# One retention / conformer / ConvFFN layer on one core: the opening goes by pairs of channel tiles, with the conditioning weights stationary, and VectorE takes 40 low parts of weights

## What is computed

```
mod  = silu(cond) @ ada_w + ada_b            # 6 x 1024 numbers for c, 6 x 1024 for c_ctx
h    = rms_norm(x, n1_pre) * (1 + sc1) + sh1 # scale and shift: the first 2 x 1024 columns of ada_w
proj = h @ w_in                              # q k v g | u_a u_b | two gates
ret  = bidirectional retention(q, k, v), per-head GroupNorm, silu(g) * ., @ ret_w_out
conv = depthwise conv 31 over u_a * sigmoid(u_b), LayerNorm, silu, @ conv_w_out
x    = x + g1 * rms_norm((sig * ret + sig * conv) @ w_mix_out, n1_post)
h2   = rms_norm(x, n2_pre) * (1 + sc2) + sh2
up   = depthwise conv 3 (h2 @ ffn_w_up);  x = x + g2 * rms_norm((silu(a) * gl) @ ffn_w_down, n2_post)
```

## Time and profile before

| | us |
|---|---|
| median of 3 runs | 2124.91 (2122.43 to 2125.99) |
| the profiled execution | 2129.53 |
| its span | 2127.7 |
| PE busy | 2082.3 (98%) |
| DVE busy | 1681.1 (79%) |
| POOL busy | 963.2 (45%) |
| ACT busy | 827.5 (39%) |

### The profile page before, as it was taken

One profiled execution on the slowest core, in us unless ns is written; L12 is line 12 of the kernel. 1 busy time (PEld: TensorE's weight loads), 2 busy tenths in 40 slices (PEclk: granted clock), 3 DMA queues, 4 the chain that ended last, 5 costly groups with the idle time before them and its releaser, 6 DMA issues.

```text
span 2127.7 us, 30742 instructions
## 1 busy us (share of the span) xinstructions
PE 2082.3 (98%) x12055; PEld 1880.9 (88%) x12055; DVE 1681.1 (79%) x1906; ACT 827.5 (39%) x1378; POOL 963.2 (45%) x597
## 2 busy tenths in 40 slices
PE   7999999999999999999999999999999999999998
PEld 3888887887887899999999998899999999978886
DVE  3599899899899687787536546599989989868867
ACT  3512212212212366665547333343433333344344
POOL 1445635645645366665381230036666566570000
PEclk9999999999999999999999999999999999999999
DMA  9342442442432455544464444312323223258453
GB/s 306 119 143 91 138 130 85 138 134 84 137 104 91 162 160 170 173 148 155 166 225 148 132 159 147 113 33 63 93 63 90 66 63 93 75 196 297 139 178 114
DMA packets 233760, 283.08 MB, mean 133 GB/s; under 512 B 11441, under 2 KB 176145, under 8 KB 233617
## 3 DMA queue, kind: packets, MB, share of 16 engines
q1 hardware_dynamic: 180785, 212.41, 31.7%
q10 hardware_dynamic: 51424, 63.98, 9.0%
q0 software_dynamic: 1408, 4.72, 0.6%
HBM read 214.06 MB, written 67.01 MB: 132 GB/s over the span
## 4 chain that ended last, share of the span: by engine, by line
PE 84%; DVE 9%; ACT 2%; issue 1%; DMA 1%; SPq 1%; POOL 1%; ACTq 0%; DVEq 0%; POOLq 0%
PE ps L1130 82%; DVE conv_y L2586 2%; DVE f_cv L2921 1%; DVE T_raw L2876 1%; SPq L766 1%; PE ps L1345 1%; DMA x_all<-in_x_sample 1%; DVE T_lo L2902 1%; DMA r_raw<-rT_d 0%; PE ps L1393 0%; DMA sh_row<-gain_d 0%; DVE Al L2960 0%; ACT sq_t L1668 0%; DVE x_all L2529 0%; PE ps L1184 0%
## 5 line engine op out<-in xcount | busy, mean ns | idle before, releaser
L2586 DVE SCALAR_TENSOR_TENSOR conv_y<-u_in,VC,conv_y 128x1167 f32<-128x1167 f32 x240 | 482.0, 2010 | 10.6 <-ACT conv_y L1759 3.6
L1130 PE MATMUL ps<-A_hi,Wa_hi 128*128 128x384 f32 x768 | 261.4, 340 | 0.5 <-DVE A_lo L2543 0.5
L2288 POOL TENSOR_TENSOR Wa_lo<-W_raw,Wa_hi 128x1024 fp32r<-128x1024 f32 x58 | 156.7, 2708 | 225.8 <-ACT Wa_hi L1637 225.7
L1130 PE MATMUL ps<-A_hi,Wa_lo 128*128 128x384 f32 x768 | 258.9, 337 | 0.0
L1130 PE MATMUL ps<-A_lo,Wa_hi 128*128 128x384 f32 x768 | 258.7, 337 | 0.0
L2921 DVE SCALAR_TENSOR_TENSOR f_cv<-f_in,VF,f_cv 128x1023 f32<-128x1023 f32 (+1 forms) x176 | 212.9, 1260 | 1.8
L2440 POOL TENSOR_TENSOR O_lo<-E,O_hi 128x512 fp32r<-128x512 f32 x80 | 130.2, 1628 | 152.6 <-ACT O_hi L1637 152.6
L2440 POOL TENSOR_TENSOR O_lo<-F_raw,O_hi 128x512 fp32r<-128x512 f32 x68 | 112.2, 1652 | 145.2 <-ACT O_hi L1637 145.2
L1130 PE MATMUL ps<-Wb_hi,A_lo 128*128 128x512 f32 x432 | 169.8, 393 | 0.0
L1130 PE MATMUL ps<-Wb_hi,A_hi 128*128 128x512 f32 x432 | 169.6, 393 | 0.0
L1130 PE MATMUL ps<-Wb_lo,A_hi 128*128 128x512 f32 x432 | 169.4, 392 | 0.0
(11 more groups left out here) (338 smaller groups left out, 5533.5 us busy)
## 6 DMA issues: line engine op xcount, KB each, us to landing
F_raw<-in_ffn_w_up SPq DMA_DIRECT2D x44, 512.0 KB, 5.6
qt<-qkvg_d SPq DMA_DIRECT2D x36, 512.0 KB, 3.6
W_raw<-in_w_in SPq DMA_DIRECT2D x32, 512.0 KB, 4.8
W_raw<-in_w_in SPq DMA_DIRECT2D x64, 256.0 KB, 3.3
ada_w<-in_ada_w ACTq DMA_DIRECT2D x30, 512.0 KB, 4.0
F_raw<-in_ffn_w_down SPq DMA_DIRECT2D x30, 512.0 KB, 4.9
A_raw<-g_d SPq DMA_DIRECT2D x25, 512.0 KB, 4.3
g_d<-f_cv SPq DMA_DIRECT2D x22, 576.0 KB, 3.6
```

The lines of the kernel that those rows point to most:

```text
L1130: return pe.matmul(out, l, r, start=start, stop=stop)
L2288: return pool.tensor_tensor(dst, x, Fv(hi), ALU.subtract)
L2586: dve.scalar_tensor_tensor(out=y, in0=x, scalar=tap, in1=y, op0=ALU.mult, op1=ALU.add).then_inc(q.conv_step, 1)
```

## The change

**Conditioning.** `ada_p` is now stationary: for one channel tile k and one of shift or scale, 8 products of 128x128 weights with `cs` (2 columns) give the column of `mod` straight in PSUM. 16 such columns make 128 products in place of 64, and `mod_row`, its copies and its turns go. It is done by pairs p of channel tiles: `ada_early(p)` is 32 products. The weights of a pair come as two DMAs of 1 MB (scale, then shift).

**Order of the steps.** A pair has 6 steps: three thirds of x times two channel tiles (`step_of`). Each step multiplies with chunk 0 and chunk 1 at once. `ada_early(p + 1)` stands after the third step of pair p. The squares and the norming of thirds 1 and 2 stand ahead of steps 2 and 4 on ACT and DVE, and `x_turn(j + 2)` ahead of the products of step j on PE. All turns use one PSUM bank, and ACT writes to three SBUF buffers; DVE makes all high and low parts.

**Queues.** SP: c, third 0 of x, chunks 0 and 1, pair 0, thirds 1 and 2, pairs 1 to 3, chunks 2 to 5. The 13 small loads go from SP to ACT's queue, behind the Silu. The exponentials of the decay go behind the splits of chunks 0 and 1.

**Low parts.** VectorE makes 40 that POOL made: chunks 6i+2 to 6i+5 for i = 1 to 7 (for odd i between taps of tile i - 1, for even i after them), and operands o = 0 to 11 of the FFN. POOL's other low parts wait for these by the counter.

```diff
-            def ada_early(n):
...
-                    last = mm(ps[0:2, n // 2, (n % 2) * 256:(n % 2 + 1) * 256], cs[:, k, :], ada_p[:, n, k, :], k == 0, k == KT - 1)
...
+            def ada_early(p):
+
+                if p:
+                    pe.wait_ge(q.mod_ok, p)
+                for v in (SC1, SH1):
+                    pe.wait_ge(*ada_piece_in(v, p))
+                    for k in (2 * p, 2 * p + 1):
+                        c = 2 * (v * KT + k)
+                        for r in range(KT):
+                            last = mm(ps[:, MOD_BANK, c:c + 2], ada_p[:, v * KT + r, k * P:(k + 1) * P], cs[:, r, :], r == 0, r == KT - 1)
+                        last.then_inc(q.ada_used, 1)
...
+                for j in range(N_A):
+                    while turned < min(j + 3, N_A):
+                        x_turn(turned)
+                        turned += 1
+                    if j < N_A - 2:
+                        for e in range(2):
...
+                            product(e, j)
+                    if j % PER_PAIR == PER_PAIR - 4 and j // PER_PAIR + 1 < N_PAIR:
+                        ada_early(j // PER_PAIR + 1)
...
             for j in range(N_A):
+                if j % PER_PAIR == 0:
+                    act.wait_ge(q.mod_ok, j // PER_PAIR + 1)
+                if j in (2, 4):
+                    squares(j // 2)
                 modulated(j)
...
+                    if i % 2 == 0 and w in LO_TAPS:
+                        if w == LO_TAPS[0]:
+                            dve.wait_ge(q.w_lo, 6 * (i + 1) + 2)
+                        lo_w(6 * (i + 1) + 2 + LO_TAPS.index(w))
...
+                    if i + 1 < KT:
+                        dve.wait_ge(q.w_lo, 6 * (i + 1) + 2)
+                        for e in range(2, 6):
+                            lo_w(6 * (i + 1) + e)
```

More of the change, by code:

```diff
@@ L826, in chunk_load @@
                                      w_in_s[:, 2 * j:2 * j + 2, 2 * g + s, h * 256:(h + 1) * 256]).then_inc(done, 16)
-            for n in range(4, 7):
-                ada_chunk(n)
             chunk_load(0)
-            ada_chunk(7)
+            chunk_load(1)
+            ada_pair(0)
             x_load(1)
-            chunk_load(1)
             sp.wait_ge(x_in[0], X_IN[0])
@@ L835, in _ @@
             sp.dma_start(x_all[:, NL, :], a["x_prompt"][0]).then_inc(x_in[2], 16)
+            for p in range(1, N_PAIR):
+                ada_pair(p)
             for n in range(2, 6):
@@ L1151, in row_turns @@
                 pe.wait_ge(q.vec_ok, 1)
-                pe.transpose(ps[:, 7, 0:120], rows[0:120, 0, :], ident[0:120, 0:120]).then_inc(q.vecT, 1)
+                pe.transpose(ps[:, ROW_BANK, 0:120], rows[0:120, 0, :], ident[0:120, 0:120]).then_inc(q.vecT, 1)
                 pe.transpose(ps[:, 5, 0:88], rows[0:88, 1, :], ident[0:88, 0:88]).then_inc(q.vecT, 1)
@@ L1205, in ada_part @@
                     last.then_inc(q.ada_used, 1)
[L1206 to L1217, removed]
-            def first_u():
[L1222 to L1243, removed]
@@ new lines, in _, with product @@
+            row_turns()
+            ada_early(0)
+            def first_u():
+                turned = 0
+                pe.wait_ge(q.vec_ok, 6)
+                def product(e, j):
+                    g, k = step_of(j)
+                    tiles = slice(3 * g, 3 * g + 3)
+                    o = ps[:, 3 * e + g, 0:TG].rearrange("p (t n) -> p t n", n=P)
+                    wh, wl = (x[chunk_slot(e)].rearrange("p (k n) -> p k n", k=KT) for x in (w_hi, w_lo))
+                    pe.wait_ge(q.hT_lo, j + 1)
+                    mm(o, wh[:, k, :], A_hi[:, tiles, k, :], k == 0, False)
+                    mm(o, wh[:, k, :], A_lo[:, tiles, k, :], False, False)
+                    return mm(o, wl[:, k, :], A_hi[:, tiles, k, :], False, k == KT - 1)
+                for j in range(N_A):
[4 more added lines that the diff above has]
+                        for e in range(2):
+                            if j == 0:
+                                pe.wait_ge(q.w_lo, e + 1)
+                            product(e, j)
+                    if j % PER_PAIR == PER_PAIR - 4 and j // PER_PAIR + 1 < N_PAIR:
+                        ada_early(j // PER_PAIR + 1)
+                for e in range(2):
+                    for j in (N_A - 2, N_A - 1):
+                        last = product(e, j)
+                    last.then_inc(q.u_ps, 1)
@@ L2315, in _ @@
                 h, g = divmod(i, 2)
-                for e in range(2, 6):
-                    if i:
-                        lo_w(6 * i + e)
                 if i:
@@ L2566, in _, with mods @@
-            for j in range(N_A):
-                if j == 3:
-                    normed(1)
-                if j == 8:
-                    meaned(2)
-                    normed(2)
+            decay_tables()
+            def mods(p):
+                dve.wait_ge(q.ada_used, 4 * (p + 1))
+                dve.wait_ge(q.vec_ok, 2)
+                two = slice(2 * p, 2 * p + 2)
+                for v in (SH1, SC1):
+                    r = v * KT + 2 * p
+                    c = 2 * r
+                    ins = dve.tensor_tensor(mod[:, r:r + 2, :], ps[:, MOD_BANK, c:c + 4].rearrange("p (k c) -> p k c", c=2),
+                                            col2(V_ADAB + r, 2), ALU.add)
+                then(ins)
+                dve.scalar_tensor_tensor(out=hscale[:, two, :], in0=mod[:, SC1 * KT + 2 * p:SC1 * KT + 2 * p + 2, :], scalar=1.0,
+                                         in1=col2(V_N1PRE + 2 * p, 2), op0=ALU.add, op1=ALU.mult).then_inc(q.mod_ok, 1)
@@ L3082, in _ @@
             t_op(R4, R4, b_of(B_lo, 1, 0), ALU.add)
+            for x in (U_S2, U_S3, U_A22):
+                op_lo(op_no(PLAIN, x))
             T_lo_part(2)
```

224 lines of the change are left out of this document (110 added, 114 removed).

## The result

The changed kernel takes 2164.32 us (median of 5 runs, 2161.51 to 2166.35) against 2125.51 of the kernel before beside it: **1.0182 times the time, 95% interval 1.0170 to 1.0194**, 38.8 us more. The forecast was 2131.1, with a range up to 2152.

The account below looks back on a forecast made before the run. PE, busy 98% of the span, was taken as the bound, so lateness at the opening's end stays. Opening +13.6, convolution -3.8 and FFN entry -3.6 gave +6.2 on 2124.91, so 2131.1 us, 8-in-10 range 2118 to 2152.

Parts of the forecast that it names:

- (2): Opening, conditioning block 0: starts at half clock, 32 records by 0.22 to 24 us, second half at full clock, ends near 27.
- the conditioning products: Opening, PE: 256 records at 0.11 us at full clock, 7.0 a block; three blocks, 21 us, stand between products, unhidden.
- 0.14 more: Price of a weight load at half clock: 0.33 instead of 0.19, from which a record was put at about 0.22 us.
- the clock falls inside the blocks: Rival, opening: PE counts as resting in conditioning blocks; 16 for three blocks, 5 for block 0, total 2152; chance 0.22.
- (3): Opening, up to the first product: scale, squares, root, norming and turn take 9.7 us together; first product near 37.
- (4): Opening, steps 0 and 1 run at half clock while third 2 of x is prepared; step 2 starts near 47.
- (5): Rest of opening: 22 steps 30.4, three blocks 21, waits and half clock 4; ends at 102 against 88.6, 13.6 later.
- The rest of this edit costs nothing that shows.: Opening: ACT's 13 DMA issues and later last four chunks cost nothing; removed row copies and turns are already counted.
- The convolution, -3.8: 28 low parts moved to DVE: PE's 2.16 wait near 659 goes, with 1.5 to 1.7 of half clock behind it.
- The FFN entry, -3.6: 12 low parts moved to DVE shorten the chain to PE's 3.64 stall at 1436; 3.6 us gained, ends 1 and 5.3.
- for each: FFN entry: DVE pays 0.6 to 0.68 us for each low part it takes over in the chain before PE's stall.
- the chances: Odds given to forecast and rival cases, forecast 0.42 (2126 to 2137); summed as faster 0.18, same 0.27, slower 0.55.

## Why the prediction was wrong, step by step

**(2) and the conditioning products: the step that failed.** The prediction ran the three inner blocks, and the second half of block 0, at full clock: 7.0 us a block, 21 for the three. They took 31.7, and block 0 took 13.7 in place of 10, because the granted clock fell in them, or did not rise. The same clock held the products behind the blocks for up to 5 us each. The first matmul of 512 columns came at 126.2 for 102, 24 too late: 10.7 of it in the three blocks, 6.1 in the five steps behind them, and 3.7 in block 0, together 20.5 of clock. With 128 moving columns in these products, 17 of it came back. The price of a record was right, 0.10 at full clock and 0.20 at half for 0.11 and 0.22, though the 0.22 does not follow from "0.14 more", which gives 0.25. (Block 0's records are 0.21 apart to its end, though the clock row of that window says 1.00; with 128 columns the same block takes 9.8.) Block 0 ended at 31.7, not 27. Of these 4.7, 1.0 is its later start: the turns of the small rows stand ahead of it, and the rows landed at 16.9.

**The rival** *the clock falls inside the blocks* was the right mechanism, with 0.22 as its chance, and nearly the right price: 16 for the blocks and the products behind, 5 for block 0. In the trace the block at 55.4 was at half clock throughout (+6.5) and the others for part of their time (+2.2 and +2.0), and the products behind them cost 2.4, 2.4 and 1.3 more. Together 17, and 3.7 for block 0. That the sums are so near is in part luck, since the rival had the three blocks alike. Its 2152, and the end of the range, still lie 12 below the 2164.3. The rest is 3 more in the opening, 4.1 of late loads, 1.7 that the low parts gave less than the forecast when measured alone, 2.7 by which the parts do not add up, and 0.6 of the other median for the kernel before.

**(3) and (4).** First product at 42.9 for 37, step 2 at 52.8 for 47: 5.9 too late, 4.7 of it block 0. The chain squares, root, norming, turn had its right length (9.9 us from the first product to step 2, for 10), but I treated it as given; moving it under block 0 brought the end of the opening 12.3 earlier.

**(5), the waits.** Allowed: 4 for waits and for the half clock behind the wait for third 2. Measured: 3.0 and 1.2. The sum is right, but by luck. Neither of the two causes that I named ends a wait of PE there: there is none at a new pair and none on ACT's splits. PE waits on DVE's low halves beside POOL's subtractions, at 116 to 125, and at the end 0.18 on ACT. That the new SBUF buffers expose DVE to POOL was in no term. From step 2 to the end it is 73.4 for 55.4, and 16.8 of these 18 are the clock in and behind the three blocks.

**"The rest of this edit costs nothing that shows."** Wrong by 4.1. SP's queue waits for the last half, and the loads of the next tile stand behind that wait; with the last halves later against PE's last products, the loads came 2.9 later against the first matmul of 512 columns.

**The convolution, -3.8.** Right in size: 3.4 measured alone, with an interval of 1.5 to 5.3. But the wait did not go, as I had said it would: 0.92 of it stays. The wait gave 1.24, and about 1.5 is the half clock that followed it in the profile of before and that does not follow it in each execution.

**The FFN entry, -3.6.** Right in kind, high by a third or more: 2.3 by the ratios, 1.8 to 2.5 in the traces. The stall fell to 1.45, not quite to the 1 of the forecast. Of the two small waits that appeared, the 0.81 on DVE's own low part belongs to the edit: the term that I paid "for each" came back as a wait. The 0.50 does not, since the new opening alone has 0.51 there with the low parts on POOL.

The sum of the parts by their ratios: +41.7 by the opening (some 4 of it the late loads), -5.7 by the low parts, 36.0; together they measured 38.7. The 2.7 between lie inside the intervals.

One slip stands in the chances: by the shares given to the cases, slower had 0.22 and eleven twelfths of 0.42, which is 0.60 and not 0.55.

## What to carry to other kernels

A long stretch that fills PE with weight loads and moves hardly any columns may run at half clock, and the products behind it too, so price it at both clocks. Here three ways out were tried: giving it columns (16 us back), cutting it in short pieces (9), and putting half of it where PE waits for data anyway. Before moving work out of a stretch that waits for DMA, ask what hid it there: the old opening's 28 us of conditioning ran while the data came, and the chain that ended last goes through a transfer of x up to 42.7 us. When a stage's last step comes closer to the next stage, look for the queue that waits on that step and what is queued behind the wait. And when a buffer moves from PSUM to SBUF, look at what its readers run beside.

## What the runs showed of the hardware

- A plain fp32 product with 128x128 stationary weights and 2 moving columns is two records of 0.10 us each at full clock and 0.20 to 0.21 at half; with 128 moving columns a record is 0.112 (7.15 for 64). In the blocks with 2 columns the granted clock fell from 1.00 to 0.50 with PE at 100% busy; with 128 columns it stayed at 1.00, and where the second block began at 0.50 it rose 3.1 us in.
- The clock row read 1.00 in block 0 of the changed kernel, up to 32 us, with records 0.21 apart. With 128 columns it read 1.00 in all of block 0 too, where 25 records took the first 5.0 us and 42 the next 4.5. In the first tens of us the spacing of the records is the better clock.
- DVE's subtraction of 128x384 took 0.56 us beside a POOL subtraction when one operand was in PSUM, and 1.45 to 2.29 when both were in SBUF (0.56 alone).
- Behind one and the same stall of PE the clock falls in one execution and not in another: near 1910 and 1950 it read 0.66 and 1.00, behind the 2.2 us on `ada_l` 0.69 before and 1.00 with the new opening alone. That is 1.5 to 2 us each, at stalls that no edit need touch, and two profiles may differ by it. Between the same two matmuls behind the convolution (672 and 1395 in the kernel before) the profiles here take 720.5 to 724.9 us.
